# Loading the input projection's weights from ACT's DMA queue instead of SP's

## The reference

```
mod = (silu(c) @ w_ada + b_ada)            # c: 9 rows of 1024; w_ada: 1024 x 6144
sh1, sc1, g1, sh2, sc2, g2 = split(mod, 6)
h = rmsnorm(x, norm1) * (1 + sc1) + sh1
u = h @ w_in                                # w_in: 1024 x 2560, five blocks q, f, i, g, v
o_a, S = hgrn2_mix(q, f, i, g, ...)         # chunkwise gated recurrence, 4 heads
o_b    = pool_mix(v, ...)                   # windowed means, then w_pool per group
x = x + g1 * (concat(o_a, o_b) @ w_out)
h2 = rmsnorm(x, norm2) * (1 + sc2) + sh2
x = x + g2 * moe(h2, w_router, w_gu, ...)   # top 4 of 32 experts
```

## Time and profile before

| | us |
|---|---|
| median of 3 launches | 2465.11 (2464.22 to 2471.11) |
| the profiled execution's own time | 2463.71 |
| its span, from the first to the last instruction | 2462.1 |
| PE busy | 2197.2 (89%) |
| DVE busy | 1608.4 (65%) |
| ACT busy | 1262.2 (51%) |

### The profile page before, as it was taken

How to read it: one execution, slowest core, us unless ns; L and a number is a source line. 1 busy time by engine, 2 the same in 40 slices (tenths; PEclk the granted TensorE clock), 3 DMA queues, 4 the chain that set the end, 5 groups by cost and what they waited for, 6 DMA issues and landing times. The chain is left out here.

```text
span 2462.1 us, 38930 instructions
## 1 busy us (share of the span) xinstructions
PE 2197.2 (89%) x12106; PEld 1594.7 (65%) x12107; DVE 1608.4 (65%) x2237; ACT 1262.2 (51%) x1660; POOL 665.8 (27%) x936
## 2 busy tenths in 40 slices
PE   3989999999985499999999899999999999999745
PEld 2767776666943367667676567777676677776431
DVE  2344554544224578778786668988797797997447
ACT  0223333333211457658665558777676676775432
POOL 2223323332231313222221123342232233241100
PEclk7999999999576699999999999999999999999875
DMA  9490000000021879779787678998898797997416
GB/s 374 183 313 16 34 34 34 34 32 28 7 68 40 305 296 320 273 275 343 263 320 272 231 241 301 382 337 327 288 377 298 271 390 275 383 361 287 149 31 232
DMA packets 144059, 555.61 MB, mean 226 GB/s; under 512 B 20864, under 2 KB 35469, under 8 KB 109605
## 3 DMA queue, kind: packets, MB, share of 16 engines
q1 hardware_dynamic: 118319, 497.22, 52.3%
q0 software_dynamic: 23680, 51.82, 9.3%
q10 hardware_dynamic: 1982, 5.45, 0.6%
HBM read 513.36 MB, written 41.25 MB: 225 GB/s over the span
## 5 line engine op out<-in xcount | busy, mean ns | idle before, releaser
L1693 DVE TENSOR_TENSOR lo<-raw,hi 128x1024 fp32r<-128x1024 f32 x800 | 932.7, 1221 | 195.9 <-ACT hi L1621 194.6
L1621 ACT ACTIVATE hi<-raw 128x1024 fp32r<-128x1024 f32 x800 | 795.2, 1049 | 143.5 <-PE pg L1566 142.8
L1563 PE MATMUL pg<-hi,xs 128*128 128x512 f32 x1056 | 424.1, 402 | 1.2 <-DVE lo L1693 1.2
L1564 PE MATMUL pg<-lo,xs 128*128 128x512 f32 x1056 | 418.5, 396 | 0.0
L1566 PE MATMUL pg<-hi,xs 128*128 128x512 f32 x1056 | 333.4, 397 | 0.0
L1563 PEld LDWEIGHTS pg<-hi,xs 128*128 128x128 f32 x1056 | 200.2, 190 | 75.7 <-issue 26.6
L1566 PEld LDWEIGHTS pg<-hi,xs 128*128 128x128 f32 x1056 | 199.6, 189 | 48.3
L1564 PEld LDWEIGHTS pg<-lo,xs 128*128 128x128 f32 x1056 | 200.1, 189 | 46.0 <-issue 0.3
L330 PE MATMUL X<-hT,w_in 128*128 128x128 f32 (+1 forms) x1728 | 225.4, 290 | 0.8 <-issue 0.8
L1491 PE MATMUL py<-hi,aT 128*128 128x512 f32 x528 | 219.4, 416 | 5.5 <-ACT aT L1633 5.5
L330 PEld LDWEIGHTS X<-hT,w_in 128*128 128x128 f32 x1728 | 220.8, 209 | 1.2 <-issue 1.2
(11 more groups left out here) (307 smaller groups left out, 2793.6 us busy)
## 6 DMA issues: line engine op xcount, KB each, us to landing
raw<-in_w_gu SPq DMA_DIRECT2D x268, 1024.0 KB, 9.5
raw<-in_w_down SPq DMA_DIRECT2D x132, 1024.0 KB, 8.3
w_out<-in_w_ada SPq DMA_DIRECT2D x12, 2048.0 KB
w_in<-in_w_in SPq DMA_DIRECT2D x5, 2048.0 KB, 20.1
moe_rows<-small SPq DMA_DIRECT2D x9, 512.0 KB, 6.5
x<-in_x_prompt SPq DMA_DIRECT2D x8, 512.0 KB, 3.5
xr<-in_x_prompt SPq DMA_DIRECT2D x8, 512.0 KB, 3.6
w_out<-in_w_out SPq DMA_DIRECT2D x1, 4096.0 KB, 15.0
```

The lines of the kernel that those rows point to most:

```text
L1563: pe.matmul(pg[u][b][:, :], xs[:, kt, 0, :], wh[:, u, :], start=False, stop=False)
L1564: pe.matmul(pg[u][b][:, :], xs[:, kt, 0, :], wl[:, u, :], start=False, stop=False)
L1621: act.activation(hi[q % RING][:, :, :], grain(q % GRAINS), ACT.Copy).then_inc(s["hi"], 1)
L1693: dve.tensor_tensor(lo[q % RING][:, :, :], grain(q % GRAINS), hi[q % RING][:, :, :].bitcast(F32), ALU.subtract).then_inc(s["lo"], 1)
```

## The change

The five loads of `w_in`, and the loads of `w_pool` and `w_rt` (the router's weights), are taken out of SP's stream and put into ACT's, behind its five small loads and ahead of its first activation. Order and sizes of the blocks stay: 1, 0, 4, 2, 3. Nothing else moves.

```
@@ block.sync
             panel(0)
             panel(1)
             sp.dma_start(x[:, :], a["x_prompt"][0, 0:P, :]).then_inc(s["x_in"], 16)
-            load_in(1)
             panel(2)
             panel(3)
-            for j in (0, 4, 2, 3):
-                load_in(j)
-            sp.dma_start(w_pool[:, :, :], a["w_pool"][0].rearrange("g c d -> c g d")).then_inc(s["w_pool"], 16)
-            sp.dma_start(w_rt[:, :, :], a["w_router"][0].rearrange("(k p) n -> p k n", p=P)).then_inc(s["w_rt"], 16)
             for p in range(FIRST, FIRST + 2):
                 panel(p)
@@ block.scalar
             act.dma_start(b_rt[:, :], a["b_router"].broadcast_to([P, E])).then_inc(s["rows_in"], 16)
+            w_in_view = a["w_in"][0].rearrange("(k p) n -> p k n", p=P)
+            for j in (1, 0, 4, 2, 3):
+                act.dma_start(w_in[:, :, j * HW:(j + 1) * HW], w_in_view[:, :, j * HW:(j + 1) * HW]).then_inc(s[f"w_in{j}"], 16)
+            act.dma_start(w_pool[:, :, :], a["w_pool"][0].rearrange("g c d -> c g d")).then_inc(s["w_pool"], 16)
+            act.dma_start(w_rt[:, :, :], a["w_router"][0].rearrange("(k p) n -> p k n", p=P)).then_inc(s["w_rt"], 16)
             act.wait_ge(s["c_in"], 32)
             act.activation(sig, c9, ACT.Sigmoid).then_inc(s["c_sig"], 1)
```

More of the change, by code:

```diff
@@ L203, in _ @@
         def _(sp):
-            w_in_view = a["w_in"][0].rearrange("(k p) n -> p k n", p=P)
             ada_view = a["w_ada"][0].rearrange("(k p) n -> p k n", p=P)
@@ L213, in panel @@
                 sp.dma_start(bada[j], a["b_ada"][0:1, n * 512:(n + 1) * 512].broadcast_to([NC, 512])).then_inc(s[f"ada_in{j}"], 16)
-            def load_in(j):
-                sp.dma_start(w_in[:, :, j * HW:(j + 1) * HW], w_in_view[:, :, j * HW:(j + 1) * HW]).then_inc(s[f"w_in{j}"], 16)
             sp.dma_start(c9[0:1, :], a["c_prompt"]).then_inc(s["c_in"], 16)
```

## The result

The changed kernel takes 2493.5 us (median of 4 launches, 2492.04 to 2497.7), the kernel before 2466.43 on the same chip (4 launches). The ratio is 1.0119, 95% interval 1.0104 to 1.0134: 25.7 to 33 us slower, 27.1 by the medians. The forecast was 2490.

The account below looks back on a forecast made before the run. The projection's start sets the end, behind a chain of conditioning rows, four panels and two rows read back. Panels +26.7, rows -1.5, clock 0 make 25.2 on 2463.71: 2488.9 profiled, median 1.4 above, 2490 us; range 2478 to 2498.

Parts of the forecast that it names:

- The forecast's own bounds: Whole kernel: ACT -3/+2, rows -2.5/+1.5, a panel's latency 0/+1.5, clock +/-2 us, written as 2484 to 2496.
- When is ACT free?: ACT's start: its seven load issues end at 41 in place of 3.3 us, 7.3 before `w_rt` lands at 48.
- The operand and panel 2: After ACT's hold: conditioning operand `cT` ready at 46 us, panel 2 issued at 50.9 in place of 19.36.
- Panels 2 and 3: PE before the projection: panel 2 multiplied at 59.0, panel 3 at 64.1 in place of 37.4 us, +26.7.
- The row of panel 6 in tile 0: Tile 0: nearest row for a panel meeting idle engines, issued 104.00, multiplied 112.08; gives panel 2 its 8.1 us.
- The rows read back: After panel 3's eviction: two rows return faster, only panels 4 and 5 beside them; -1.5 us, bounds 0 and 4.
- The clock: PE at the projection's start: same idle time before it, granted clock 0.50 as before; 0, with 2 us either way.
- Everything moves together afterwards: After the projection's start: later loads are issued on semaphores of DVE and PE, so nothing is caught up.
- the first (ACT not held, sharing alone): Rival at the start: ACT's queue isn't held, SP's gets half the rate; `ada(3)` near 50, +15 us, 2480; chance 0.10.
- The rule of the Trainium skill: DMA issue on several engines: saves only sequencer time, usually small; change worth about nothing, 2465 in place of 2490.

Follow-up runs that it names:

- The version with both held back: The changed kernel, but SP issues panels 4 and 5 only when the two modulation rows have landed; 2488.68 us, ratio 1.0103.
- the one that lets the rows through on SP's queue: Kernel before, all loads on SP: block 1 behind panels 2 and 3, other blocks and small weights only after the two modulation rows land; ratio 1.001.
- the wait alone: Kernel before, all loads on SP, with one wait for block 1 of the input weights added ahead of ACT's first sigmoid; 2474.81 us, ratio 1.0046.
- The version with the sigmoid first: The changed kernel, but ACT's first two activations stand ahead of the seven loads; 2484.87 us, ratio 1.0079.

## Why the prediction was right

The mechanism and nearly every step of the sum came out. The number fell 3.5 us short: 1.9 of it in the difference (25.2 forecast, 27.1 by the medians), 1.3 in the kernel before, whose median with its fourth launch is 2466.43 in place of 2465.11, the rest rounding. The forecast's own bounds add up to 2482.5 to 2497, not to the 2484 to 2496 written there; the measured time lies in both.

1. *When is ACT free?* Forecast 41 by counting 17.0 MB and taking off the 7.3 us; measured 40.62. The seven issues took 1.1, 4.2, 10.8, 8.6, 5.0, 5.0 and 2.45 us. `w_rt` landed 9.7 us after its issue began, as before: at 47.9, where 48 was forecast.
2. *The operand and panel 2.* Forecast 46 and 50.9; measured 45.66 (45.43 + 0.23) and 50.70.
3. *Panels 2 and 3.* Forecast 59.0 and 64.1; measured 58.74 and 63.94, +26.6. The row of panel 6 in tile 0 priced a load into idle engines to 0.3 us.
4. *The rows read back.* Forecast -1.5; measured from the eviction's end at 68.83 to 79.53, 10.70 against 10.22: +0.5. This term failed. I took panels 4 and 5 to be light traffic. They aren't: the store of panel 3 is issued at 68.86 and panel 5 at 68.90, so the rows share the engines with a whole panel; from 68.8 to 79.5 SP's queue moves 2.85 MB, against 3.17 before from 42.2 to 52.5. The version with both held back shows 6.25, and the one that lets the rows through on SP's queue 6.22. So the traffic is the price, and it was present in both kernels.
5. *The clock.* Counted 0 with 2 us either way. The projection's first 192 products took 24.51 in place of 23.27, +1.2, with a granted clock of 0.52 over its first 6.2 us against 0.73 over the same stretch before. PE had idled for 15 us before them in both kernels; that the low stretch lasted longer here is seen, not explained. It isn't tied to the hold: the wait alone shows 0.51 there, and one block on ACT 0.62. Terms 4 and 5 together, 3.2 us, bring 25.2 to 28.4, which is the shift seen at tile 0.
6. *Everything moves together afterwards.* The table above says so for eleven versions.

Of the rivals, the first (ACT not held, sharing alone) gave 50 for panel 3 and 2480. The version with the sigmoid first shows that half of it exists, panel 3 at 49.62, but ACT is held there too. In the changed kernel the sharing made no panel late by itself, since both first panels had landed long before the operand was there; its part is inside the hold, which lasts until SP's 4.7 MB have passed too. The rule of the Trainium skill ("DMA: Bandwidth & Descriptors", "Issuing engines are not separate DMA queues"), by which only the issue time of a sequencer is at stake and is usually small, fails on this case by its second half: the issue time was 37.3 us, on the stream that the chain began with. Its first half, that both queues run on the same engines and interleave, agrees with 1019 packets against 1018.

## What to carry to other kernels

A DMA queue isn't free for the stream that feeds it. Before bulk loads are put on a computing engine's queue, count what will be in flight when each is issued and ask what that engine does next; here the first 2 MB load was taken in 1.1 us and the second in 4.2, and from the third on the stream stood still for 5.0 to 10.8 us a load, the pace at which earlier ones drained. Where the DMA engines are full anyway, a second queue brings no bytes sooner (409 GB/s with two, 407 with one): what pays is the order of the transfers, by when each is needed, and there the small transfer at the very end of the list can be the next bound, as the second tile's rows were.

## What the runs showed that I had not expected

- A hold isn't even: the third issue took 10.8 us and the fifth 5.0. While two queues share the engines, each drains at half the rate, and so a held stream stands twice as long for the same bytes.
- The two modulation rows, 1 MB with their stores, cost 10.0 to 11.5 us beside bulk traffic, over nine versions with before, and 6.2 to 6.5 without, in three.
- The cost isn't proportional to the blocks moved. At tile 0 one block on ACT costs 1.2 us, two 4.7, three 9.4 and all seven loads, the bytes of 5.2 blocks, 28.3. The launches say the same more coarsely: 6.4 us (3.7 to 9.1) for two, 7.9 (4.9 to 10.8) for three, 29 (25.7 to 33) for all.
